# Two projections with tokens on partitions, their norm taken per tile of 128 tokens and turned back on TensorE

## The reference

```
x = x + rms_norm(mix @ w_out, attn_post_g)          # norm n2
h2 = rms_norm(x, ffn_pre_g)                         # norm n3
f = conv_ffn(h2, w_up, conv_w, conv_b, w_down)      # 1024 -> 8192 -> 4096 -> 1024
x = x + rms_norm(f, ffn_post_g)                     # norm n4
z = rms_norm_2(x, norm_gain) @ w_in                 # norm n5
rms_norm(v, g) = v * rsqrt(mean(v*v) + 1e-6) * g    # over the features of one token
```

## Time and profile before

| | |
|---|---|
| median of 3 runs (lowest to highest) | 1407.51 us (1405.44 to 1407.89) |
| the profiled execution, its time and span | 1406.38 us, 1404.1 us |
| mean granted TensorE clock | 0.977 of full speed |
| busy: TensorE, VectorE, ScalarE, GpSimd | 1331.5, 856.3, 579.7, 229.6 us |
| packets' bytes, mean rate | 116.48 MB, 83 GB/s |

### The profile page before, as it was taken

One profiled execution on the slowest core, in us unless ns is written; L12 is line 12 of the kernel. 1 busy time (PEld: TensorE's weight loads), 2 busy tenths in 40 slices (PEclk: granted clock), 3 DMA queues, 4 the chain that ended last, 5 costly groups with the idle time before them and its releaser, 6 DMA issues.

```text
span 1404.1 us, 16192 instructions
## 1 busy us (share of the span) xinstructions
PE 1331.5 (95%) x6006; PEld 1038.5 (74%) x6006; DVE 856.3 (61%) x1471; ACT 579.7 (41%) x848; POOL 229.6 (16%) x181
## 2 busy tenths in 40 slices
PE   7999988899999999999999999899799989999996
PEld 6776655688888888888888767687578856657885
DVE  6455753788887388648843523669987256653342
ACT  5345554544433243224412434413564246554231
POOL 2322220000000000000000324320005411114451
PEclk9999999999999999999999999799899999999999
DMA  5211101132222222322232131311122210002411
GB/s 190 90 61 60 61 30 60 34 116 90 90 102 107 90 90 93 117 90 90 90 113 96 61 121 64 146 60 60 60 90 90 93 59 31 31 31 69 166 66 60
DMA packets 17785, 116.48 MB, mean 83 GB/s; under 512 B 1984, under 2 KB 2240, under 8 KB 4544
## 3 DMA queue, kind: packets, MB, share of 16 engines
q1 hardware_dynamic: 16320, 108.35, 21.7%
q10 hardware_dynamic: 1408, 7.37, 1.4%
HBM read 111.52 MB, written 4.19 MB: 82 GB/s over the span
## 4 chain that ended last, share of the span: by engine, by line
PE 81%; DVE 14%; ACT 3%; issue 2%; DMA 1%; ACTq 0%; DVEq 0%; SPq 0%
PE PG L337 20%; PE PG L339 20%; PE PG L338 20%; PE PX L424 4%; PE PX L699 3%; PE PX L608 2%; PE PG L728 2%; PE PX L738 1%; DVE MD L1584 1%; DVE XC L1610 1%; DVE WL L1208 1%; DVE MD L1602 1%; PE PX L373 1%; DVE SM L1599 1%; PE PX L541 1%
## 5 line engine op out<-in xcount | busy, mean ns | idle before, releaser
L317 POOL TENSOR_TENSOR WL<-RAW,WH 128x512 fp32r<-128x512 f32 x168 | 226.3, 1378 | 1141.9 <-ACT WH L786 1141.9
L337 PE MATMUL PG<-XH,WH 128*128 128x512 f32 x992 | 392.8, 396 | 17.0 <-DVE WL L1208 9.3
L338 PE MATMUL PG<-XL,WH 128*128 128x512 f32 x992 | 387.9, 391 | 0.0
L339 PE MATMUL PG<-XH,WL 128*128 128x512 f32 x992 | 387.9, 391 | 0.0
L786 ACT ACTIVATE WH<-RAW 128x2048 fp32r<-128x2048 f32 x100 | 191.4, 1914 | 386.4 <-PE PG L339 375.4
L337 PEld LDWEIGHTS PG<-XH,WH 128*128 128x128 f32 x992 | 187.4, 189 | 64.4 <-DVE WL L1208 11.9
L338 PEld LDWEIGHTS PG<-XL,WH 128*128 128x128 f32 x992 | 187.5, 189 | 39.7 <-issue 1.4
L339 PEld LDWEIGHTS PG<-XH,WL 128*128 128x128 f32 x992 | 187.3, 189 | 39.5
L1208 DVE TENSOR_TENSOR WL<-RAW,WH 128x2048 fp32r<-128x2048 f32 x58 | 132.6, 2287 | 19.3 <-ACT WH L786 19.1
L337 PE MATMUL PG<-AH,WH 128*128 128x512 f32 x256 | 99.6, 389 | 0.0
L338 PE MATMUL PG<-AL,WH 128*128 128x512 f32 x256 | 99.6, 389 | 0.0
(11 more groups left out here) (292 smaller groups left out, 1967.8 us busy)
## 6 DMA issues: line engine op xcount, KB each, us to landing
RAW<-panels SPq DMA_DIRECT2D x100, 1024.0 KB, 4.8
...
```

What stands on the lines that cost most here:

```text
L317: ins = pool.tensor_tensor(WL[:, s].rearrange("p a b -> p (a b)")[:, piece], RAW[:, s, piece], WH[:, s].rearrange("p a b -> p (a b)")[:, p ...
L337: pe.matmul(o, WH[:, s, c, ms], xh[:, c, :], start=(c == 0), stop=False)
L338: pe.matmul(o, WH[:, s, c, ms], xl[:, c, :], start=False, stop=False)
L339: mm = pe.matmul(o, WL[:, s, c, ms], xh[:, c, :], start=False, stop=(c == DC - 1))
```

## The change

The output projection and the four down projections are computed the other way round: the activations are the stationary operand and 512 columns of weights move, so that a result tile has 128 tokens on partitions and 512 features along the free dimension (`out_pass`, `down_panel`; Y4 and F4 hold them). The number and width of the gemm's matmuls stay. A down panel is now a quarter of the weights, by half of the input and half of the output, and its results are taken out of PSUM after every second panel.

A token's sum of squares is then a sum along the row. ScalarE squares a half row with a running sum (`half_squares`) and takes a root; VectorE makes the factor of each of the tile's tokens, with one Newton step (`token_factor`). Tiles 0 and 1 are scaled by ScalarE and turned by TensorE with the identity; tiles 2 and 3 are turned by a matmul with a diagonal of the factors, DG. The turned chunks lie in six banks of PSUM; chunks 6 and 7 are turned inside the next stage's panel 0. `post` has two operations per chunk. The matmuls with O1024 and `keep_warm` are gone for n2 and n4. The first two low parts of in2a go from GpSimd to VectorE.

```diff
+LO_ON_DVE[FIRST["in2a"][0]] = LO_ON_DVE[FIRST["in2a"][0] + 1] = True
...
+BANKS = {"n2": [PX[:, 1, :], PX[:, 0, :], PX[:, 2, :], PG[:, 1, :], PX[:, 3, :], PG[:, 0, :]],
+         "n4": [PX[:, 0, :], PX[:, 1, :], PX[:, 2, :], PX[:, 3, :], PG[:, 0, :], PG[:, 1, :]]}
...
+            if chunk_done is not None and m == 1 and c < 2:
+                chunk_done(c)
...
+    def down_panel(q, k):
+        p = FIRST[f"dn{q}"][0] + k
+        f, half = divmod(k, 2)
+        pe.wait_ge(w_lo, p + 1)
+        if half == 0:
+            pe.wait_ge(evac, p - 2)
+        for t in range(NB):
+            o = PG[:, (t + 2) % NB, :] if f else PX[:, t, :]
+            ts = slice(t * P, (t + 1) * P)
+            for c in range(4):
+                wh, wl = (w[:, p % 2].rearrange("p a b -> p (a b)")[:, c * S:(c + 1) * S] for w in (WH, WL))
+                ah, al = (a[:, q % 2, 4 * half + c, ts] for a in (AH, AL))
+                pe.matmul(o, ah, wh, start=(half == 0 and c == 0), stop=False)
+                pe.matmul(o, al, wh, start=False, stop=False)
+                mm = pe.matmul(o, ah, wl, start=False, stop=(half == 1 and c == 3))
+            if half == 1 and t < NB - 1:
+                mm.then_inc(once("dn_tile"), 1)
+        mm.then_inc(panel_done, 1)
+    def turn_back(norm, y, c, tiles):
+        for t in tiles:
+            o = BANKS[norm][c][:, t * P:(t + 1) * P]
+            src = y[:, t, c * P:(c + 1) * P]
+            if t < 2:
+                mm = pe.transpose(o, src, IDN[:])
+            else:
+                mm = pe.matmul(o, src, DG[:, t - 2, :], start=True, stop=True)
+        if NB - 1 in tiles:
+            mm.then_inc(once("tok_turned"), 1)
+    def turn_all(norm, y, last_out):
+        pe.wait_ge(once("tok_scaled"), 2 * TURN[norm] + 2)
+        for c in range(4):
+            turn_back(norm, y, c, (0, 1))
+        pe.wait_ge(once("tok_factor"), 4 * TURN[norm] + 3)
+        for c in range(4):
+            turn_back(norm, y, c, (2,))
+        turn_back(norm, y, 4, (0, 1, 2))
+        last_out()
+        turn_back(norm, y, 5, (0, 1, 2))
+        pe.wait_ge(once("tok_factor"), 4 * TURN[norm] + 4)
+        for c in range(6):
+            turn_back(norm, y, c, (3,))
+    def turn_rest(norm, y, new):
+        def chunk_done(c):
+            pe.wait_ge(once(new), c + 1)
+            turn_back(norm, y, 6 + c, range(NB))
+        return chunk_done
...
+        wh, wl = (w[:, s].rearrange("p a b -> p (a b)")[:, (c - c0) * S:(c - c0 + 1) * S] for w in (WH, WL))
+        xh, xl = (x[:, c, t * P:(t + 1) * P] for x in (XH, XL))
+        pe.matmul(o, xh, wh, start=(c == c0), stop=False)
+        pe.matmul(o, xl, wh, start=False, stop=False)
+        return pe.matmul(o, xh, wl, start=False, stop=(c == c0 + 3))
...
-    acc, sq = once("n2_acc"), once("n2_sq")
-    for t in range(4):
+    for t in range(NB):
         if t == 1:
             pe.wait_ge(evac, p - 1)
         if t == 3:
             pe.wait_ge(evac, p)
-            pe.wait_ge(acc, 1)
-            pe.matmul(PX[:, 1, :], O1024[:], SQY[:, 0, :], start=True, stop=False)
-            pe.matmul(PX[:, 1, :], O1024[:], SQY[:, 1, :], start=False, stop=False)
         o = PX[:, (0, 2, 3)[t], :] if t < 3 else PG[:, 0, :]
         for c in range(4, DC):
             mm = out_pass(o, p, t, c, 4)
         mm.then_inc(once("y1_tile") if t < 3 else panel_done, 1)
-    for t in range(2):
-        pe.wait_ge(sq, 4 + t)
-        mm = pe.matmul(PX[:, 1, :], O1024[:], SQY[:, 6 + t, :], start=False, stop=(t == 1))
-    mm.then_inc(once("n2_sum"), 1)
-    keep_warm(30)
+    turn_all("n2", Y4, lambda: pe.wait_ge(evac, FIRST["out1"][0] + 4))
...
-    gemm_norm("up0", "n3", SQY, "x2_split")
+    gemm_norm("up0", "n3", SQY, "x2_split", chunk_done=turn_rest("n2", Y4, "x2_new"))
...
-        if q < 3:
-            gemm(f"dn{q}", AH[:, q % 2], AL[:, q % 2])
+        for k in range(4):
+            down_panel(q, k)
         if nxt:
             gemm(nxt)
-    gemm_sums("dn3", "n4", SQF, AH[:, 1], AL[:, 1])
+    turn_all("n4", F4, lambda: pe.wait_ge(evac, FIRST["dn3"][0] + 4))
...
+    gemm_norm("in2a", "n5", SQF, "x3_split", {1: w_idx, 2: kv_sums, 3: ln_sums, 4: turns},
+              turn_rest("n4", F4, "x3_new"))
...
+    def half_squares(norm, y, t, f, dump):
+        act.activation(dump[:, 4 * f + t, :], y[:, t, f * S:(f + 1) * S], ACT.Square,
+                       accum_out=(SSB if f else SSA)[:, t:t + 1]).then_inc(once("tok_sum"), 1)
+    def token_factors(norm, y, last_out, dump, ahead):
+        for t in range(NB):
+            if t < 3:
+                act.wait_ge(once("tok_y"), 3 * TURN[norm] + t + 1)
+            else:
+                act.wait_ge(*last_out)
+            half_squares(norm, y, t, 1, dump)
+            if t == 0:
+                act.wait_ge(once("tok_half"), TURN[norm] + 1)
+            act.wait_ge(once("tok_sum"), 8 * TURN[norm] + 5 + t)
+            act.activation(MSR[:, t:t + 1], SSB[:, t:t + 1], ACT.Sqrt, bias=MSV[:, t:t + 1], scale=1.0 / 1024)\
+                .then_inc(once("tok_root"), 1)
+            if t < 2:
+                act.wait_ge(once("tok_factor"), 4 * TURN[norm] + t + 1)
+                act.activation(y[:, t, :], y[:, t, :], ACT.Copy, scale=RTK[:, 3 * t + 2:3 * t + 3])\
+                    .then_inc(once("tok_scaled"), 1)
+        hi_ahead(ahead)
...
-    act.activation(SQY[:, 7, :], Y1[:, 7, :], ACT.Square).then_inc(sq, 1)
-    hi_ahead(FIRST["out1"][0] + 3)
-    factor("n2", R[:])
+    act.preload_act_table_set("sqrt_and_others")
+    for t in range(NB):
+        if t % 2 == 0:
+            act.wait_ge(*((once("y1_out"), 1) if t == 0 else (evac, FIRST["out1"][0] + 3)))
+        half_squares("n2", Y4, t, 0, SQY)
+    token_factors("n2", Y4, (evac, FIRST["out1"][0] + 4), SQY, FIRST["out1"][0] + 3)
...
-    hi_squares("dn3", "n4", SQF, FA)
-    factor("n4", R[:])
+    p0 = FIRST["dn3"][0]
+    act.preload_act_table_set("sqrt_and_others")
...
+    hi_ahead(p0 + 2)
+    token_factors("n4", F4, (evac, p0 + 4), SQF, p0 + 3)
...
+    def first_half(norm):
+        dve.wait_ge(once("tok_sum"), 8 * TURN[norm] + NB)
+        dve.tensor_scalar(MSV, SSA, 1.0 / 1024, EPS, ALU.mult, ALU.add).then_inc(once("tok_half"), 1)
+    def token_factor(norm, t):
+        v, r = MSV[:, t:t + 1], [RTK[:, 3 * t + k:3 * t + k + 1] for k in range(3)]
+        dve.wait_ge(once("tok_root"), 4 * TURN[norm] + t + 1)
+        link(dve.reciprocal(r[0], MSR[:, t:t + 1]))
+        link(dve.scalar_tensor_tensor(out=v, in0=SSB[:, t:t + 1], scalar=1.0 / 1024, in1=v,
+                                      op0=ALU.mult, op1=ALU.add))
+        link(dve.scalar_tensor_tensor(out=r[1], in0=r[0], scalar=v, in1=r[0], op0=ALU.mult, op1=ALU.mult))
+        link(dve.tensor_scalar(r[1], r[1], -0.5, 1.5, ALU.mult, ALU.add))
+        if t < 2:
+            dve.tensor_tensor(r[2], r[0], r[1], ALU.mult).then_inc(once("tok_factor"), 1)
+        else:
+            dve.tensor_scalar(DG[:, t - 2, :], IDN[:], r[0], r[1], ALU.mult, ALU.mult).then_inc(once("tok_factor"), 1)
...
-    lo_ahead(p)
-    for t in range(4):
+    for t in range(NB):
         if t < 3:
             dve.wait_ge(once("y1_tile"), t + 1)
         else:
             dve.wait_ge(panel_done, p + 2)
-        dve.tensor_tensor(Y1[:, 4 + t, :], PX[:, (0, 2, 3)[t], :] if t < 3 else PG[:, 0, :], PROJ[:, 14 + t, :], ALU.add)\
-            .then_inc(once("y1_out") if t < 3 else evac, 1)
...
-    lo_ahead(p + 1)
-    def post(name, y, cname, new, hi_name, lo_name, gain):
-        dve.wait_ge(once(name + "_r"), 1)
+        dve.tensor_tensor(Y4[:, t, S:], PX[:, (0, 2, 3)[t], :] if t < 3 else PG[:, 0, :], PROJ[:, 14 + t, :], ALU.add)\
+            .then_inc(once("tok_y") if t < 3 else evac, 1)
+        if t == 0:
+            first_half("n2")
+            lo_ahead(p)
+        token_factor("n2", t)
+    def post(norm, cname, new, hi_name, lo_name, gain, ahead):
+        for c in range(DC + 1):
             if c < DC:
-                step_(dve.scalar_tensor_tensor(out=y[:, c, :], in0=y[:, c, :], scalar=col(cname, c),
-                                               in1=R[:], op0=ALU.mult, op1=ALU.mult))
-                dve.tensor_tensor(XT[:, c - 1, :], XT[:, c - 1, :], y[:, c - 1, :], ALU.add).then_inc(once(new), 1)
-            if c >= 3:
-                k = c - 3
+                dve.wait_ge(once("tok_turned"), 8 * TURN[norm] + c + 1)
+                dve.scalar_tensor_tensor(out=XT[:, c, :], in0=BANKS[norm][c], scalar=col(cname, c),
+                                         in1=XT[:, c, :], op0=ALU.mult, op1=ALU.add).then_inc(once(new), 1)
+            if c >= 1:
+                k = c - 1
                 dve.wait_ge(once(hi_name), k + 1)
                 dve.scalar_tensor_tensor(out=XL[:, k, :], in0=XT[:, k, :], scalar=col(gain, k),
                                          in1=XH[:, k, :].bitcast(F32), op0=ALU.mult, op1=ALU.subtract)\
                     .then_inc(once(lo_name), 1)
```

(7 more changed lines are left out.)

110 lines of the change are left out of this document (72 added, 38 removed).

## The result

The changed kernel took 1396.68 us (median of 7 executions, 1391.46 to 1399.97), the kernel before 1405.44 us beside it (7, 1402.71 to 1407.89): a ratio of 0.9934, 95% interval 0.9912 to 0.9956, some 9 us faster. The forecast was 1400.2, from 1396.8 to 1405.3; the median lies 0.1 us under the range.

The account below looks back on a forecast made before the run. TensorE, busy 95% of the span, bounds the kernel, so only its waits at norms n2 and n4 can shrink: -3.7 - 6.3 + 2.7 (clock) = -7.3 us, from 1407.5 to 1400.2 us, range 1396.8 to 1405.3.

Parts of the forecast that it names:

- The gemm step: Matmuls of out1 and the down stages, operands swapped: step stays 0.23 us, no change in time.
- The chain of factors at n2: From ScalarE's split at 230.15, tile factors 3.1 us apart, first chunk at 249.3; slower than TensorE's tiles every 2.7 us.
- `post` and what follows: After n2's first chunk: two operations per chunk gain 4.7 us, the WL gives 1.0 back; net at n2 -3.7 us.
- n4: Norm after dn3: first chunk at 789.2, last XT 7.3 us earlier, WL gives 1.0 back; net -6.3 us.
- The base: Time of the kernel before from which the forecast counts: the median of its runs, 1407.5 us.
- The clock: Without `keep_warm`, TensorE's gaps at n2 and n4 lower the clock: +1.35 us per norm, +2.7 in all.
- The prediction's -3.2 us: Sum for the whole change by the skill's advice alone, with two clock falls at each norm.
- The table load: At n2 ahead of the squares: next activation starts 1.29 us after the load; by the skill's page 1.4 us later.
- Dearer small operations: Rival: some 19 chained steps per norm cost 0.30 us each, not 0.20; 3.8 us in all, 1404.0; chance 0.15.
- The shift taken back: Rival: the earlier first panel only waits longer for the means of n3 and n5; no change, 1407.5; chance 0.06.
- The clock that stays down: Rival: turning at both norms puts the clock into a long stay at half, costing 13.8 us; 1411.3; chance 0.10.
- The clock that holds: Rival: TensorE is kept going enough or falls where it waits anyway; sum -10.0 us, 1397.5; chance 0.17.

Follow-up runs that it names:

- interleave: Changed kernel with VectorE's add and ScalarE's square and root of the next tile ahead of this tile's factor and copy, WL first; 1391.15 us, ratio 0.9895.
- lo_pool: Changed kernel with the second panel's WL behind each of the two norms made by GpSimd instead of VectorE; 1397.71 us, ratio 0.9945.
- warm: Changed kernel with idle matmuls ahead of the turned tiles, behind the last, and ahead of both means; 1393.49 us, ratio 0.9918.
- n2_warm: Kernel before with the change at out1 and n2 only, plus idle matmuls in three places of that norm; 1402.27 us, ratio 0.9971.

## Why the prediction was right or wrong, point by point

**The gemm step** was right: 389 ns per matmul on the page, no wait at the starts of the down and up stages.

**The chain of factors at n2** was right: out1's last matmul starts at 240.03 (forecast 240.9 in the old times, and this execution reached A 0.70 earlier), the factors begin 3.15, 3.14 and 2.90 apart (3.1), and the first chunk is read 19.08 us behind A (forecast 249.3 - 230.15 = 19.15). One slip in the working did no harm: the wait of 1.34 and the means of 1.4 ahead of out1's last tile add up to 2.7, while the forecast takes 3.3 off, and out1's last matmul did move from 13.84 to 10.58 behind A, 3.26. The claim that it runs late against TensorE is what interleave shows.

**`post` and what follows**: 1.32 us per chunk (1.33), and last XT, XL, WL, sums in the forecast order; the WL's 1.0 us is confirmed by lo_pool. TensorE waits 2.06 us ahead of the means (2.3). From the split to the second panel it is -3.87 in the profile (forecast -3.7); A to B, free of falls in warm and n2_warm, is -3.9.

**n4**: -6.42 (forecast -6.3). First chunk 6.1 us behind dn3's last matmul, as worked out (789.2 - 783.12).

**The base** is the step that failed: "From the median of 1407.5 the forecast is 1400.2". The forecast is 3.5 us above the measured time. Of these 2.1 are the base: three executions gave 1407.51, seven gave 1405.44 beside the changed kernel, and the three comparisons behind it 1405.4 to 1406.1. Another 1.2 are the clock (below), and 0.3 the two norms, -10.3 where -10.0 was forecast. On the base of 1405.44 the same terms and bounds would have given 1398.1 and a range from 1394.7 to 1403.2, with the measured 1396.68 inside. As a difference, -7.3 with bounds of -10.7 and -2.2, the forecast holds: measured were -8.8 and -8.2 in the two comparisons. The kernel before runs from 1401.4 to 1408.3 over its 50 executions in the comparisons of the experiments, and two of the three of the base, 1407.51 and 1407.89, lie near its top: bad luck in a small draw. The profiled execution, 1406.38 at a known clock, was the better base, with 1399.1 and a lower bound of 1395.7. The range took nothing for this: it had no term for what the falls of an execution do to a median of three.

**The clock** is the term whose size was off, +1.35 per norm, +2.7 in all. In the profile it is +1.6 at n2 and 0 at n4, though both norms have the same gap of 2.06 us ahead of the means. By the times it is what is left between -10.3, the norms free of falls, and the measured -8.8 and -8.2: +1.5 and +2.1. By the lost part it is less: over all executions the changed kernel loses 34.3 us against 31.8 of before, 2.5 more, and if each execution has the fall of 1.7 in which TensorE waits, 0.8 of that is paid. So the term was 0.8 to 2.1, not 2.7. The prediction's -3.2 us takes two falls at each norm; there are two at n2, of which the first costs nothing, and none at n4. That number was the prediction's own reading: the Trainium skill, "TensorE: Matmul & The Clock Gate", section "Why this matters for your kernels", advises against idle gaps from a certain length on, and counts no falls. The Trainium skill, "TensorE: Matmul & The Clock Gate", section "What's actually happening", states that the same kernel varies from run to run in how many matmuls run cold; the 13 executions of the changed kernel agree: spans of 1389.3 to 1398.3 at clocks of 0.980 to 0.972.

**The table load** at n2 cost 1.28 to 1.44 us on the path (1.29 in the working). The next activation starts 1.30 after it (table load at 231.39, square at 232.69), so the second part of the price that the Trainium skill, "ScalarE: Activation LUTs", section "What ACT_TABLE_LOAD costs", adds for a drain isn't seen; the load itself agrees.

**The rivals.** Dearer small operations: no, the steps within a factor are 0.19 to 0.25. The shift taken back: no. The clock that stays down: no; 786 to 800 is at full clock, and the fall at n2 is over by 248 (1.00 from 247 to 248). The clock that holds: half of it, at n4.
